# A dense attention's border in two parts of the tokens, with one combined factor for two norms

## The reference

```python
# end of the first model
h = h + conv_ffn(...)                    # layer 1's feed-forward
x = rms_norm(h, final_norm)
# begin of the second
h = rmsnorm(x, norm1_g[0]) * (1.0 + sc1) + sh1
qkv = h @ w_qkv                          # then rotary embedding of q and k, attention, w_o
x = x + g1 * y
```

## Time and profile before

| | |
|---|---|
| median of 3 runs | 2778.66 us (2778.28 to 2780.54) |
| profiled execution, own time | 2779.12 us |
| its span | 2777.1 us |
| PE busy | 2730.6 us, 98% |
| DVE busy | 1734.1 us, 62% |
| ACT busy | 1031.2 us, 37% |
| POOL busy | 136.0 us, 5% |
| mean granted PE clock | 0.995 |

### The profile page before, as it was taken

The page is one execution under the profiler, slowest core; times in us unless marked ns, Lnnn a source line. Parts: engine busy times, 40 slices in busy tenths (PEclk is TensorE's granted clock), DMA queues, the critical chain, the costliest instruction groups (busy, mean ns, idle before and its releaser), DMA issues.

```text
span 2777.1 us, 35595 instructions
## 1 busy us (share of the span) xinstructions
PE 2730.6 (98%) x14468; PEld 2218.1 (80%) x14468; DVE 1734.1 (62%) x2550; ACT 1031.2 (37%) x1503; POOL 136.0 (5%) x171
## 2 busy tenths in 40 slices
PE   7999999999999999999899999999999999999999
PEld 6888788888876688888775788887887888888887
DVE  4388677474677477464757667575664988643434
ACT  4245444242435444232435543232332222432322
POOL 0000200000023200000003300000000000000000
PEclk9999999999999999999999999999999999999999
DMA  5532134343322134343320036453331111332221
GB/s 167 120 74 65 46 127 151 115 151 95 90 76 82 60 120 152 121 141 94 97 76 16 18 118 208 140 195 127 122 119 57 35 35 32 107 120 91 91 84 53
DMA packets 262619, 276.84 MB, mean 100 GB/s; under 512 B 23800, under 2 KB 231160, under 8 KB 262457
## 3 DMA queue, kind: packets, MB, share of 16 engines
q1 hardware_dynamic: 232264, 219.51, 25.4%
q10 hardware_dynamic: 30192, 55.05, 6.3%
HBM read 267.19 MB, written 7.34 MB: 99 GB/s over the span
## 4 chain that ended last, share of the span: by engine, by line
PE 93%; DVE 4%; ACT 2%; issue 1%; DMA 0%; SPq 0%; ACTq 0%; DVEq 0%
PE ps L572 26%; PE ps L574 25%; PE ps L573 25%; PE ps L1273 3%; PE ps L1305 2%; PE ps L884 2%; PE ps L1032 2%; PE ps L1049 1%; PE ps L1230 1%; PE ps L1251 1%; PE ps L1066 1%; PE ps L1138 1%; PE ps L630 1%; PE ps L1117 1%; PE ps L1183 0%
## 5 line engine op out<-in xcount | busy, mean ns | idle before, releaser
L572 PE MATMUL ps<-sb 128*128 128x512 f32 (+2 forms) x3460 | 1290.1, 373 | 11.6 <-DVE sb L1990 2.5
L574 PE MATMUL ps<-sb 128*128 128x512 f32 (+2 forms) x3460 | 1269.7, 367 | 0.0
L573 PE MATMUL ps<-sb 128*128 128x512 f32 (+2 forms) x3460 | 1269.7, 367 | 0.0
L572 PEld LDWEIGHTS ps<-sb 128*128 128x128 f32 (+1 forms) x3460 | 653.1, 189 | 139.6 <-issue 27.5
L574 PEld LDWEIGHTS ps<-sb 128*128 128x128 f32 (+1 forms) x3460 | 652.9, 189 | 111.7
L573 PEld LDWEIGHTS ps<-sb 128*128 128x128 f32 (+1 forms) x3460 | 653.5, 189 | 108.3 <-issue 1.7
L1957 DVE TENSOR_TENSOR sb<-sb 128x2048 fp32r<-128x2048 f32 (+2 forms) x188 | 420.2, 2235 | 324.7 <-ACT sb L1391 324.7
L1391 ACT ACTIVATE sb<-sb 128x2048 fp32r<-128x2048 f32 (+2 forms) x196 | 365.0, 1862 | 273.8 <-PE ps L574 272.5
L2238 DVE SCALAR_TENSOR_TENSOR sb<-ps,sb 128x511 f32<-128x511 f32 (+1 forms) x264 | 193.6, 747 | 126.9 <-ACT sb L1641 121.7
L1641 ACT ACTIVATE sb<-ps,sb 128x512 f32<-128x512 f32 x132 | 96.0, 777 | 274.2 <-PE ps L574 274.1
L2274 DVE SCALAR_TENSOR_TENSOR sb<-sb 128x512 f32<-128x512 f32 x168 | 126.0, 750 | 12.5
(11 more groups left out here) (235 smaller groups left out, 2190.1 us busy)
## 6 DMA issues: line engine op xcount, KB each, us to landing
sb<-in_ffn_w_up SPq DMA_DIRECT2D x88, 1024.0 KB, 5.1
sb<-in_ada_w ACTq DMA_DIRECT2D x192, 256.0 KB, 3.2
sb<-in_ffn_w_down SPq DMA_DIRECT2D x32, 1024.0 KB, 5.2
sb<-in_ffn_w_down SPq DMA_DIRECT2D x16, 768.0 KB, 4.5
sb<-in_hy_w_in SPq DMA_DIRECT2D x12, 1024.0 KB, 5.2
sb<-in_hgrn_w_in SPq DMA_DIRECT2D x8, 1024.0 KB, 6.8
sb<-in_hgrn_w_in SPq DMA_DIRECT2D x16, 512.0 KB, 4.9
sb<-in_dsa_w_in SPq DMA_DIRECT2D x6, 1024.0 KB, 5.3
```

Source lines behind the costliest of these rows:

```text
L572: pe.matmul(o, al, bh, start=f, stop=False, **kw)
L573: pe.matmul(o, ah, bl, start=False, stop=False, **kw)
L574: m = pe.matmul(o, ah, bh, start=False, stop=l, **kw)
```

## The change

- Border 8 joins `NEXT` and is halved: the last item and `kk` 0 and 1 are made by halves of the tokens. Both kinds of sums of squares go to bank 7, side by side (columns 0 to 127 and 128 to 255), and all calls for both kinds are made for each half.
- h's factor comes from both sums at once: two small DVE instructions (`both_norms`), one root, one reciprocal. It is spread by `spread_pair`, two matmuls into one bank, of which the second waits for the first.
- x's own factor comes behind: its root (ACT) and reciprocal (DVE, 128x128) stand after the second half's; PE spreads it (two `spread_pair`) between the second halves of `kk` 0 and `kk` 1; DVE multiplies x by it (`first_norm`, 8 instructions) after all of h.
- The three small gain instructions move ahead of the border (`both_gains`).
- The low part of the item of `v` goes from DVE, ahead of x's update, to POOL.
- SP's program has no edit.

```diff
-NEXT = {1: ("ffn0", 1), 4: ("dsa", 0), 5: ("ffn1", 1), 10: ("ffn2", 0), 13: ("hy", 1), 14: ("ffn3", 0)}
+NEXT = {1: ("ffn0", 1), 4: ("dsa", 0), 5: ("ffn1", 1), 8: ("attn", 1), 10: ("ffn2", 0), 13: ("hy", 1), 14: ("ffn3", 0)}
+TWICE, BOTH, FIRST = 8, (4, 6), (5, 7)
...
+            def spread_pair(bank, src, name, blocks):
+                pe.wait_ge(*at("inverse", *name))
+                wait_bank(bank)
+                for n, tt in enumerate(blocks):
+                    p = slice(32 * tt, 32 * tt + 32)
+                    if n:
+                        pe.wait_ge(*at("spread", *name, blocks[0]))
+                    pe.matmul(ps[bank][:, 128 * n:128 * n + 128], ones[p, :], src[p, 0:128], start=True, stop=True, skip_group_check=True).then_inc(
+                        *mark("pe_stat", ("spread", *name, tt)))
...
             def squared_half(r, half):
+                kinds = 2 if r == TWICE else 1
                 for j in (6, 7):
-                    pe.wait_ge(*at("sq", r, 0, j, half))
-                    sums(STAT, sq[j % 2], False, j == NT - 1, (2 * half, 2 * half + 1)).then_inc(
+                    for i in range(kinds):
+                        pe.wait_ge(*at("sq", r, i, j, half))
+                        sums(STAT, (sq, ht)[i][j % 2], False, j == NT - 1, (2 * half, 2 * half + 1), 128 * i).then_inc(
...
                             if k == NT - 1:
                                 m.then_inc(*mark(sem, done[n][j], *([("used", keys[n])] if j else [])))
                                 freed[banks[n][j]] = then[n][j]
+                    if r == TWICE and n == 0:
+                        freed[FIRST[1]] = [("rms", "final"), ("sum", 1)]
+                        for half in range(2):
+                            spread_pair(FIRST[half], rb[0], ("final",), (2 * half, 2 * half + 1))
+                            freed[FIRST[half]] = [("x", 9, 7)]
...
-                for g in range(2):
-                    project("pe_attn", ("attn", "kk", g), (0, 1) if g else (2, 3), [("rot_mm", 2 * g + i) for i in range(2)],
-                            [[("rot_sq", 2 * g + i)] for i in range(2)], ready=ready)
-                    turn([2 * g, 2 * g + 1])
+                halved_start("pe_attn", TWICE, [("attn", "kk", g) for g in range(2)], ((2, 3), (0, 1)),
+                             [[("rot_mm", 2 * g + i) for i in range(2)] for g in range(2)], [[[("rot_sq", 2 * g + i)] for i in range(2)] for g in range(2)])
+                turn([0, 1])
+                turn([2, 3])
...
             def rms_half(r, half):
+                if r == TWICE:
+                    act.wait_ge(*at("sum", half))
+                    act.activation(rb[i][p, 0:128], rb[i][p, 0:128], ACTF.Sqrt, scale=1024.0).then_inc(*mark("act_stat", ("rms", stage, half)))
+                    if half:
+                        rms(rb[0][:, 0:128], STAT, D, ("stat", r, 1), ("final",))
+                    return
...
             def squares_half(r, j, half):
-                act.wait_ge(*at("sq_used", r, 0, j - 2))
-                act.activation(sq[j % 2][:, hs], x[:, j, hs], ACTF.Square).then_inc(*mark("act_sq", ("sq", r, 0, j, half)))
+                for i in range(2 if r == TWICE else 1):
+                    act.wait_ge(*at("sq_used", r, i, j - 2))
+                    act.activation((sq, ht)[i][j % 2][:, hs], x[:, j, hs], ACTF.Square, scale=v("final_norm", j) if i else 1.0).then_inc(
+                        *mark("act_sq", ("sq", r, i, j, half)))
...
             def normalise_halves(r, gain, shift, then):
+                if r == TWICE:
+                    both_norms(0)
                 inverse(rb[i][0:64, 0:128], (stage, 0))
                 added(r, 6, 1)
...
-                            elif half == 0 and k == 4:
+                            elif half == 0 and k == 3 and r == TWICE:
+                                both_norms(1)
+                            elif half == 0 and k == (5 if r == TWICE else 4):
                                 inverse(rb[i][64:128, 0:128], (stage, 1))
-                ahead(then)
+                                if r == TWICE:
+                                    inverse(rb[0][:, 0:128], ("final",))
+                if then:
+                    ahead(then)
...
+            def both_norms(half):
+                p = slice(64 * half, 64 * half + 64)
+                t = rb[NEXT[TWICE][1]][p, 0:128]
+                dve.wait_ge(*at("stat", TWICE, half))
+                dve.tensor_scalar(t, ps[STAT][p, 0:128], EPS / D, EPS * EPS, MUL, ADD).then_inc(*step("sum_first", half))
+                dve.wait_ge(*at("sum_first", half))
+                dve.scalar_tensor_tensor(t, ps[STAT][p, 128:256], 1.0 / D, t, MUL, ADD).then_inc(*mark("dve_stat", ("sum", half)))
+
+            def first_norm():
+                dve.wait_ge(*at("spread", "final", 3))
+                own = banks8[:, FIRST[0]:FIRST[1] + 1:2, 0:256]
+                two = lambda t: t.rearrange("p (a q) -> p a q", a=2)
                 for j in range(NT):
-                    dve.scalar_tensor_tensor(blocks(x[:, j, :]), blocks(x[:, j, :]), v("final_norm", j), factor_2, MUL, MUL).then_inc(*mark("dve_x", ("x", 9, j)))
+                    dve.scalar_tensor_tensor(two(x[:, j, :]), two(x[:, j, :]), v("final_norm", j), own, MUL, MUL).then_inc(*mark("dve_x", ("x", 9, j)))
...
-            end_and_modulated()
+            dve.wait_ge(*at("g1", "attn", 2))
+            normalise_halves(TWICE, lambda j: g1c[:, j:j + 1], 0, None)
+            first_norm()
...
             def attention():
+                low_weight(("ffn1", "down", len(GROUPS) - 1, 3))
                 scale("attn", T)
```

More of the change, by code:

```diff
@@ L625, in project_tokens, with sums @@
                 return m
-            def sums(bank, squares, first, last, of=range(4)):
+            def sums(bank, squares, first, last, of=range(4), c=0):
                 for tt in of:
-                    m = pe.matmul(ps[bank][32 * tt:32 * tt + 32, 0:128], ones[:, 0:32], squares[:, 128 * tt:128 * tt + 128],
+                    m = pe.matmul(ps[bank][32 * tt:32 * tt + 32, c:c + 128], ones[:, 0:32], squares[:, 128 * tt:128 * tt + 128],
                                   start=first, stop=last, skip_group_check=True)
@@ L649, in spread_half @@
                 blocks = (2 * half, 2 * half + 1)
+                if stage == "attn":
+                    spread_pair(BOTH[half], rb[i], ("attn", half), blocks)
+                    freed[BOTH[half]] = [("t", stage, half, 7)]
+                    return
                 spread(0, i, (stage, half), blocks)
@@ L652, in spread_half @@
                     freed[FB[tt]] = [("t", stage, half, 7)]
+            def spread_pair(bank, src, name, blocks):
[7 more added lines that the diff above has]
+                        *mark("pe_stat", ("spread", *name, tt)))
             def squared_half(r, half):
+                kinds = 2 if r == TWICE else 1
                 for j in (6, 7):
-                    pe.wait_ge(*at("sq", r, 0, j, half))
-                    sums(STAT, sq[j % 2], False, j == NT - 1, (2 * half, 2 * half + 1)).then_inc(
-                        *mark("pe_stat", ("sq_used", r, 0, j, half), *([("stat", r, half)] if j == NT - 1 else [])))
+                    for i in range(kinds):
+                        pe.wait_ge(*at("sq", r, i, j, half))
+                        sums(STAT, (sq, ht)[i][j % 2], False, j == NT - 1, (2 * half, 2 * half + 1), 128 * i).then_inc(
+                            *mark("pe_stat", ("sq_used", r, i, j, half), *([("stat", r, half)] if j == NT - 1 and i == kinds - 1 else [])))
             def halved_end(sem, r, key, banks, ready, tile, squared):
@@ L775, in squared @@
                         if j is None:
-                            wait_bank((STAT, OTHER)[i])
+                            if i == 0:
+                                wait_bank(STAT)
                             pe.wait_ge(*at("acc", r, i, 3))
@@ L779, in squared @@
                             pe.wait_ge(*at("sq", r, i, j))
-                        sums((STAT, OTHER)[i], (ht if i else sq)[1 if j in (None, 5, 7) else 0], j is None, j == NT - 1).then_inc(
+                        sums(STAT, (ht if i else sq)[1 if j in (None, 5, 7) else 0], j is None and i == 0, j == NT - 1, c=128 * i).then_inc(
                             *mark("pe_stat", ("sq_used", r, i, j), *([("stat", r, i)] if j == NT - 1 else [])))
@@ L1149, in dsa @@
                 end("pe", "dsa")
[L1151 to L1156, removed]
             def attention():
@@ L1773, in dsa @@
                 end("act", "dsa")
[L1775 to L1780, removed]
             def attention(before):
@@ L1927, in act_program @@
             ffn(1, "dsa")
-            end_and_modulated()
+            normalise(TWICE, ("ffn1", "down", len(GROUPS) - 1, 3), 0)
             attention("ffn1")
@@ L2021, in normalise_halves @@
                     pieces = lambda t: t.rearrange("p (t q) -> p t q", t=2)
-                    dve.wait_ge(*at("spread", stage, half))
```

(9 more changed lines are left out.)

1 line of the change is left out of this document (added).

## The result

The kernel after takes 2783.49 us (median of 20 runs, 2782.07 to 2786.38), the kernel before 2778.39 us (20 runs): ratio 1.0019, 95% interval [1.0013, 1.0025]. It is 5.1 us slower; 5.2 were predicted. The interval alone leaves room for anything from 3.6 to 6.9 us, so a hit to 0.1 us is finer than the medians can show.

What follows compares the result with a forecast made beforehand. PE, busy 98% of the span, was taken to bound the kernel. A rotation 2.6 us later plus 2.6 us of slow clock made 5.2 us on 2778.66: 2783.9 us, range 2779.6 to 2787.2.

Steps and rivals of the forecast that it cites:

- The two terms of the sum: At the rotation behind border 8: 2.6 us later start plus 2.6 us of slow clock, 5.2 us slower.
- Part 1: First half's factor at border 8: 0.9 us added over border 13, 0.2 for the pair; first multiplication at 1359.9.
- Part 2: DVE to the end of h: 1.6 us added to border 13's 19.2 (bounds 0.6, 2.6); `v`'s high part at 1380.7.
- a credit of 1.0 us: DVE's stretch over h: border 13's wait for the second spread goes, taking off 1.0 us.
- Part 6: Clock behind PE's standstill, on the rotation and `v`: falls again, costing 2.6 us (bounds 0 and 3.4).
- Part 3: PE to the end of `kk` 1: through at 1389.1 instead of 1391.3, 2.2 us sooner.
- Part 4: x's own update on DVE, 5.35 us, ends at 1388.9: costs nothing, with 0.8 us of cover.
- Part 5: `v`'s low part on POOL ends at 1387.25, delaying tables: PE stands 4.9 us, rotation 2.6 us later; `v` itself hidden.
- the wait without the slow clock: Rival at the rotation: tables late, but the clock holds; 2.6 us slower, 2781.3 us; chance 0.2.
- hidden after all: Rival at the rotation: tables land before PE wants them; 2.2 us faster, 2776.5 us; chance 0.08.
- closes as meant: Rival: border 8 becomes like border 13 with nothing lost behind it, 8 us faster; chance 0.01.
- a figure of the Trainium skill: Halved products up to `kk` 1: columns / 2.4 GHz plus about 2.5 ns per matmul; halving costs 0.25 us, not 1.15.

Runs made afterwards that it cites:

- the first run, e1_tables_first: Kernel after, with the fence and four table loads issued on SP ahead of `q` 2's load: 2777.08 us, ratio 0.9999.
- the other two traces of a whole border: Kernel before with table loads ahead of `q` 2 (2779.45 us), and kernel before with `v`'s low part on POOL (2778.56 us).
- the last run: Kernel after with tables first, bank 0 and interleaved spreads, plus x's combined reciprocal moved behind all of h: 2776.92 us, ratio 0.999.
- the filler run, e3: Kernel after, with 20 extra 512-column matmuls on PE between `kk` 1 and the rotation: 2780.79 us, ratio 1.001.
- e8_before_pool_low: Kernel before, with only `v`'s low part moved from DVE to POOL: 2778.56 us, ratio 0.9999.
- e2_low_on_dve: Kernel after, with `v`'s low part back on DVE between h and x's update: 2778.99 us, ratio 1.0003.
- e4: Kernel before, with the fence and four table loads issued on SP ahead of `q` 2's load: 2779.45 us, ratio 1.0001.

## Why the prediction was right

The forecast's mechanism and place are confirmed: the tables behind SP's queue, by the chain of waits and by the first run. The size came out right too, but that it did to 0.1 us is partly luck, as shown below. Point by point, in before's time:

| step | predicted | measured |
|---|---|---|
| third quarter starts | 1354.4 | 1354.41 |
| first multiplication of h | 1359.9 | 1360.25 |
| `v`'s high part starts | 1380.7 | 1380.73 |
| POOL is through with its low part | 1387.25 | 1387.40 |
| `perm` has landed | 1393.95 | 1394.18 |
| PE is through with `kk` 1 | 1389.1 | 1389.8 |
| rotation starts | 1394.0 | 1394.44 |
| rotation later than before | 2.6 | 3.1 |
| price of the slow clock | 2.6 | 1.95 |
| sum | +5.2 | +5.1 (medians) |

The two terms of the sum missed by 0.5 us up and 0.65 us down, and the misses cancel. The 3.1 also hangs on the trace of before: by the other two traces of a whole border it would be 3.6 and 4.4. Behind them, three pieces were mis-sized.

- **The pair** (Part 1): 0.7 us was taken, with 1.0 as the upper bound from twice 0.49. The row of the kernel after has 1.02, over that bound. At x's two pairs 1.3 was close to the 1.54 from start to next product.

```profile
1362.11 1.02 PE L669 MATMUL ps<-sb 32*128 32x128 f32 x4 [0.18 <-DVE sb L1991]
```

- **The second half on DVE** (Part 2): the point in time was right, the reasons were not. From the first multiplication to `v`'s high part it took 20.5 us (1360.25 to 1380.73), where 19.2 + 1.6 = 20.8 were forecast; the first multiplication itself was 0.35 us late, and the two misses cancel. The reciprocal of 0.95 us was counted as delaying h; the last run shows that it does not. Beside it stood a credit of 1.0 us for no longer waiting for the second spread, and with the pair at 1.0 us instead of 0.7 that spread is again as late as DVE. The two wrong terms belonged to the same place and nearly met; the 0.3 us that are left were not taken apart.
- **The clock** (Part 6): 1.95 instead of 2.6 (the part works out 2.7 from its rows and then calls 2.6 the measured one; a slip of 0.1). The stretch was 6.9 us long, but 2.3 us of it were spent waiting (1395.0 to 1397.36), so 4.7 us of work ran slow where in the trace of before it was 5.8.

The landing took 6.8 us from the low part's end instead of 6.7 (1390.33 to 1397.10), the sequence of issues being the same, and PE started 0.25 us behind it. Part 3's 2.2 us of gain at `kk` 1's end were 1.5 against the same trace; half of what is missing is the late first multiplication, and the rest fits the longer pairs. Part 4 (x's update hidden) was right: PE never waits for it in any run. The standstill at `v` was none, as Part 5 had it.

None of the rivals came about in the kernel after. The edits bring two of their outcomes about, though not by the rivals' own mechanisms: "the wait without the slow clock" is what the filler run makes of it (2780.79 us measured, 2781.3 named), and "hidden after all" is what the first run makes of it (2777.08 measured, 2776.5 named). The gap that "closes as meant", 8 us, is not reached even there. Border 8 has a second kind of sums, the pairs and a longer wait for bank 6 (1.58 us, 0.56 at border 13); no run prices all of its excess.

Part 3 held a figure of the Trainium skill (TensorE: Matmul & The Clock Gate, "Wait — 56ns, not 53.3ns?") against the rows. The kernel after does not agree with the page and bears out the rows, with 0.12 us between 256-column matmuls in `kk` 1 (1387.10, 1387.22, 1387.34 in its timeline) at a granted clock of 1.00. No run separates the price of halving from the rest.

## What to carry to other kernels

When a change makes the bound engine reach a point sooner, or moves a step on which a queue waits, list what else stands behind that step in the queue. Here it was four small table loads, early by 4.9 us in the trace of before. A trace shows what waited; slack that is about to be spent has to be computed, as landing time against first use. A load that depends on little (here on the fence only) goes ahead of one that waits for a buffer.

## What the runs showed of the hardware

- The granted clock differs between executions of the same code well away from any change: the kernel after has stretches at half clock at 777 and 815 us, where the kernel before had 1.00 in its profile; of the edited kernels one trace had none of them (e1_tables_first), the others one or both, some of them shorter. In the kernel after and in e1_tables_first alike PE has a pause of 0.8 us shortly ahead of each of the two places; in the one the clock fell behind it, in the other it did not. The border's start differs by up to 3 us from trace to trace (1346.11 to 1349.03), as much as most effects in this study. Even the kernel before with one edit on SP, whose code up to the border is the same, began it at 1349.01. Among the halved kernels, intervals inside one trace resolved 0.6 us where medians of 11 runs did not.
- The slow stretch behind the old gap was 10.2 us long in the trace of before and 6.8 us in that of e8_before_pool_low, with the same work on PE there.
- With PE standing still for 1.86 us (e2_low_on_dve), and in another place for 1.58 (e1_tables_first), the clock stayed at 1.00; with 4.46 us it fell to half for 6.9 us. Twenty matmuls without use in that wait kept it at 1.00 and saved 1.95 us.
- Two spreading calls into one bank, of which the second waits for the first, took 1.02 us; two without the wait took 0.49. Four in two such pairs took 1.61 us, and 1.07 when the banks alternate, so that another call stands between a call and the one that waits for it.
- A load of 64 KB (`perm`) took 4.9 to 5.3 us from issue to landing behind a load of 1 MB and two of 256 KB on SP's queue (before, after, e2, e3, e8), and 2.8 and 3.9 us with only the two of 256 KB just ahead (e4, e1).
- POOL's subtraction of 128x2048 took 4.57 to 4.62 us in all nine places of the kernel after, beside a DVE busy for 1.22 of 4.6 us (at 322.7) as beside one busy for 4.29 (at 795.0).
